# Loading ScalarE's joint table of logarithm and exponential by hand, in a fused two-model block

## What is computed

```python
def rms_norm(x, g):                      # norm1, norm2, pre/post norms, norms of q and k
    y = xf * lax.rsqrt(jnp.mean(xf * xf, axis=-1, keepdims=True) + EPS)
...
def forgetting_attention(q, k, v, fg_logit):     # 8 heads of 64, causal
    log_f = jax.nn.log_sigmoid(fg_logit)
    cum = jnp.transpose(jnp.cumsum(log_f, axis=1), (0, 2, 1))
    ...
        s = s + cum[:, :, start:end, None] - cum[:, :, None, :end]
        p = jax.nn.softmax(s, axis=-1)
...
def conformer_conv(...):                 # sigmoid gate, depthwise conv, layer_norm, silu
...
# the feed-forward part: silu(gate) * val
def retention(q, k, v):                  # 8 heads; ends in a group norm: rsqrt(var + EPS)
...
def diff_attention(q, k, v, lam):        # 8 heads, two softmaxes each
    p = jax.nn.softmax(jnp.where(mask, sc, neg), axis=-1)
    w = p[:, :, 0] - lam * p[:, :, 1]
...
o = rmsnorm(o, sub_norm_b[j]) * (1.0 - lambda_init)
y = (o * jax.nn.silu(gate)) @ w_out_b[j]
```

## Time and profile before

| | |
|---|---|
| median of 3 runs | 3242.74 us (3241.93 to 3243.2) |
| the profiled execution's own time | 3246.35 us |
| its span, first to last instruction | 3244.7 us |
| mean granted TensorE clock | 0.939 of 2.4 GHz |
| TensorE matmuls busy | 2837.1 us |
| VectorE busy | 1677.9 us |
| ScalarE busy | 745.0 us |

### The profile page before, as it was taken

One profiled execution on the slowest core, in us unless ns is written; L12 is line 12 of the kernel. 1 busy time (PEld: TensorE's weight loads), 2 busy tenths in 40 slices (PEclk: granted clock), 3 DMA queues, 4 the chain that ended last, 5 costly groups with the idle time before them and its releaser, 6 DMA issues.

```text
span 3244.7 us, 35199 instructions
## 1 busy us (share of the span) xinstructions
PE 2837.1 (87%) x13202; PEld 2246.1 (69%) x13202; DVE 1677.9 (52%) x2240; ACT 745.0 (23%) x1220; POOL 110.6 (3%) x124
## 2 busy tenths in 40 slices
PE   5518999797899999998999999999977999999785
PEld 4406666486787877876788888888865777777564
DVE  5671444425545555456444544544474666666534
ACT  3224434202111111112101110111042333333321
POOL 0330000000000000000000000000000000000000
PEclk9758999798999999999999999999988999999887
DMA  3101110032434344332322222222242222222121
GB/s 137 65 0 65 53 43 34 14 143 91 143 117 151 120 160 148 118 142 93 141 78 78 78 78 90 78 78 73 83 156 81 65 68 65 65 68 65 42 104 65
DMA packets 48617, 286.58 MB, mean 88 GB/s; under 512 B 6577, under 2 KB 6705, under 8 KB 18609
## 3 DMA queue, kind: packets, MB, share of 16 engines
q1 hardware_dynamic: 22064, 119.01, 10.8%
q0 software_dynamic: 14544, 105.91, 9.5%
q10 hardware_dynamic: 11952, 60.89, 4.9%
HBM read 248.03 MB, written 29.36 MB: 85 GB/s over the span
## 4 chain that ended last, share of the span: by engine, by line
PE 77%; DVE 14%; issue 4%; ACT 3%; DMA 1%; SPq 0%; DVEq 0%; ACTq 0%
PE PB L238 11%; PE PB L239 11%; PE PB L240 11%; PE OBB L238 8%; PE OBB L239 7%; PE OBB L240 7%; PE OBB L908 5%; PE PB L868 4%; PE TBB L822 4%; DVE cacc L727 2%; PE TBB L238 2%; PE TBB L239 2%; PE TBB L240 2%; DVE small L1069 1%; DVE V L1458 1%
## 5 line engine op out<-in xcount | busy, mean ns | idle before, releaser
L238 PE MATMUL PB<-HH,WH 128*128 128x512 f32 x1520 | 601.0, 395 | 40.9 <-DVE HL L370 16.1
L239 PE MATMUL PB<-HL,WH 128*128 128x512 f32 x1520 | 595.7, 392 | 0.0
L240 PE MATMUL PB<-HH,WL 128*128 128x512 f32 x1520 | 595.3, 392 | 0.0
L238 PE MATMUL OBB<-HH,WH 128*128 128x512 f32 x992 | 404.0, 407 | 6.1 <-DVE WL L254 6.1
L239 PE MATMUL OBB<-HL,WH 128*128 128x512 f32 x992 | 389.9, 393 | 0.0
L240 PE MATMUL OBB<-HH,WL 128*128 128x512 f32 x992 | 389.9, 393 | 0.0
L238 PEld LDWEIGHTS PB<-HH,WH 128*128 128x128 f32 x1520 | 288.2, 190 | 109.3 <-issue 41.0
L239 PEld LDWEIGHTS PB<-HL,WH 128*128 128x128 f32 x1520 | 288.2, 190 | 61.7 <-issue 2.0
L240 PEld LDWEIGHTS PB<-HH,WL 128*128 128x128 f32 x1520 | 287.9, 189 | 60.8
L254 DVE TENSOR_TENSOR WL<-RAW,WH 128x2048 fp32r<-128x2048 f32 x101 | 230.7, 2284 | 69.9 <-DMA WH<-units 53.7
L1012 ACT ACTIVATE E<-PB,small 128x128 f32<-128x128 f32 (+3 forms) x192 | 142.1, 741 | 430.4 <-DVE small L1072 430.4
(11 more groups left out here) (298 smaller groups left out, 3725.1 us busy)
## 6 DMA issues: line engine op xcount, KB each, us to landing
WH<-units POOLq DMA_DIRECT2D x85, 1024.0 KB, 5.0
RAW<-units SPq DMA_DIRECT2D x85, 1024.0 KB, 4.7
gs<-units ACTq DMA_DIRECT2D x16, 1024.0 KB, 4.7
gu<-gs ACTq DMA_DIRECT2D x16, 1024.0 KB, 3.9
RAW<-gu SPq DMA_DIRECT2D x16, 1024.0 KB, 4.8
WH<-gu POOLq DMA_DIRECT2D x16, 1024.0 KB, 5.1
tmpd<-xr SPq DMA_DIRECT2D x128, 64.0 KB, 2.0
A<-xT SPq DMA_DIRECT2D x4, 1024.0 KB, 12.4
```

Of the source, the lines that this page charges most:

```text
L238: first = pe.e.matmul(out, wh, xh, start=start, stop=False)
L239: pe.e.matmul(out, wh, xl, start=False, stop=False)
L240: return pe.e.matmul(out, wl, xh, start=False, stop=stop), first
```

## The change

```diff
+LN_EXP = "natural_log_exp_and_others"
...
 def root_act(act, squares):            # norm1, norm2
...
+            act.e.preload_act_table_set(LN_EXP)
             act.e.wait_ge(pe_done, at_mark(act, "pe", "total"))
             roots(act, PB[0], rbn)
...
 def norm_a_act(act, ph):
...
             spill(act)
+            act.e.preload_act_table_set(LN_EXP)
             act.e.wait_ge(pe_done, at_mark(act, "pe", "total"))
             roots(act, TBB, rbx)
...
 def total_act(act, ph, out):           # post_a, post_b
             act.start(ph)
+            act.e.preload_act_table_set(LN_EXP)
             act.e.wait_ge(pe_done, at_mark(act, "pe", "total"))
             roots(act, TBB, out)
...
 def mix_act(act, ph):
...
                 act.e.activation(sbm[:, c, :], cacc[:, c, :], ACT.Square).then_inc(act_done, act.mark(f"csq{c}"))
+            act.e.preload_act_table_set(LN_EXP)
             act.e.wait_ge(pe_done, at_mark(act, "pe", "var1"))
             act.e.wait_ge(dve_done, at_mark(act, "dve", "cum_lo"))
...
 def attend_act(...):
...
             if not forget:
                 e.wait_ge(dve_done, at_mark(act, "dve", "rawg1", i))
                 e.activation(sg[:, :], sg[:, :], ACT.Silu).then_inc(act_done, act.mark("silu"))
+                e.preload_act_table_set(LN_EXP)
             if more:
...
 def first_act(act, ph, forget):        # both attentions
             act.start(ph)
+            act.e.preload_act_table_set(LN_EXP)
             if not forget:
                 act.e.wait_ge(pe_done, at_mark(act, "pe", f"new{KT - 1}"))
                 roots(act, OBB, rbx)
```

## The result

| | before | after |
|---|---|---|
| median of the runs beside each other (5 each) | 3242.74 us (3241.12 to 3245.73) | 3225.01 us (3222.3 to 3226.84) |
| profiled execution, its own time | 3246.35 us | 3225.01 us |
| its span, mean granted clock | 3244.7 us, 0.939 | 3223.3 us, 0.942 |

The ratio is 0.9944 [0.9929, 0.9958]: 17.7 us faster (the interval reaches from 13.6 to 23.0 us), where 18.1 were forecast. Against the profiled execution of before the gain is 21.4 us of span, because that execution was 3.6 us above its median and this one is at its own.

What follows compares the result with a forecast made beforehand. TensorE, busy 87% of the span, was taken to bound the kernel, so only ScalarE loads on the chain count: 14 loads x 1.29 = 18.1 us, from 3242.74 to 3224.6 us. The range was 3213 to 3232.

Steps and rivals of the forecast that it cites:

- The sum, 14 loads by 1.29 us, 18.1 us: Whole kernel: of the loads removed, 14 were on the path at 1.29 us each, 18.1 us in all.
- norm2, post_a, post_b, two loads each: Norms over the model width: both loads leave the path, the new one hidden under TensorE's total; 6 loads together.
- last head, two: Last differential head: no projection left, TensorE waits 5.27 us for L1885, and both loads are in that wait.
- norm1, mix and the first attention, four loads, 5.16 us: Path loads saved: norm1's exponential load, mix's L640 load, and two behind the first attention's k0 and k1 logarithms.
- norm_a, nothing: Norm_a: no gain, as the chain goes through the 17.92 us spill of A and the root is done long before.
- Attention loop, 24 loads, nothing: Attention loop: its 24 loads gain nothing, as the exponentials end 3.4 us before TensorE wants them.
- heads, 14 loads, nothing: Differential heads in the loop: 14 loads gain nearly nothing, taken as 0, at most 0.3 us in two or three heads.
- First differential head, two loads: First differential head: both loads saved, new load within 16.5 us of ScalarE idle, everything behind serial, so all should travel.
- rival 1: Gain caught by a DMA or projection in first attention, first differential head or post_a: 6 loads lost, 3232.4 us; 12%.
- The copy of q, cost 0 by 9.8 us of cover: Differential heads: the new load delays q's copy (L1059) by 1.28 us, but its readers start 9.8 us later; cost 0.
- Rival 2, the clock: TensorE's clock shifts across the loop's seven heads: 3209.6 us if all at 1.00, 3230.6 if none; same mix expected; 16%.
- Rivals 3, 4 and 5: Joint table slower, 3260.6 us (2%); loads ignored, 3242.7 (3%); a switch holding ScalarE twice its row, 3206.6 (2%).

Runs made afterwards that it cites:

- the twenty switches: Changed kernel with twenty more loads in post_b behind the wait for TensorE's sum, alternating Exp and joint table: 3249.32 us, ratio 1.0015.
- the two opposite kernels: Changed kernel with separate Ln and Exp loads only in the loops, 3224.79 us (0.9949), or only on the path, 3241.53 us (0.9997).
- the kernel with the loops' tables apart: Changed kernel with separate Ln and Exp loads again in the attention loop and the loop of differential heads: 3224.79 us, ratio 0.9949.

## Why the prediction was right

- **The sum, 14 loads by 1.29 us, 18.1 us.** Measured 17.7, and 18.3 when these 14 were put back with three beside the path. The price was tested alone, by the twenty switches (1.288 us), and which loads count by the two opposite kernels. That the total came within 0.4 us is in part luck. The interval of the measurement, 13.6 to 23.0 us, would fit 11 to 17 loads; the places one by one are the better evidence. And between the two profiled executions the rows without a load moved by -1.47, +2.45, +0.56 and +0.76 us, which the sum put at nothing.
- **norm2, post_a, post_b, two loads each; last head, two.** Right: 2.65, 3.03, 2.67 and 2.56 us. The cover of the new load in post_b is larger than the 1.28 us needed, with 2.49 us to spare; and with that cover taken away the load behind the wait costs what the text said, about one load for each place.
- **norm1, mix and the first attention, four loads, 5.16 us.** 6.80 in the two executions. The loads are gone from the chain in each place. The rest, 1.6 us, is not theirs: from norm1 to the attention's first kT, TensorE's clock is at 1.2 GHz for 128.2 us before and 123.3 after, and executions of the changed kernel's code differ there by 1.1 us among themselves (248.57 to 249.66 us).
- **norm_a, nothing.** Right: the spill is on the chain at the same distance from its surroundings.
- **Attention loop, 24 loads, nothing; heads, 14 loads, nothing.** Right within the 1.6 us by which the kernel with the loops' tables apart differs. The 2.45 us that the heads' stretch took less is not theirs, but the clock's.
- **First differential head, two loads, "so all of it should travel".** This step failed by 1.2 us up to the transposes in the profiled execution, though the clock gave as much back just behind them. The text named rotation, swaps and VectorE as serial and took their length as fixed; the first swap grew from 1.98 to 3.26 us, because it came forward into the next weight load. It is rival 1 in small, at one of its three places, and for a reason that the row would have shown: the load's issue at 2455.88 stood 6.3 us ahead of the swap in the trace of before.
- **The copy of q, cost 0 by 9.8 us of cover.** Right in its result, wrong in its reason. The text named the Square as queued behind the copy, but priced only the copy. What decides is the chain from the Square to the scaling: 6.2 us of room on average, and 1.5 us of waiting per head once 7.7 us are added; the rest of the 2.5 is clock.
- **Rival 2, the clock.** Its expectation of the same mix held for the seven heads of the loop: two of the seven heads in the loop run their 16 matmuls in 2.05 us in both kernels (other heads 3.4 to 3.8), so two at the full 2.4 GHz before and two after. They are other heads, though: after they are these of the chain, before the ones that start this piece at 2632.90 and 2868.20.

```profile
2699.09 2.05 PE OBB L913 x16
...
2934.49 2.05 PE OBB L913 x16
```

  Outside these seven the clock did move: at the edges of the heads' stretch for some 2 us of gain, in the first attention for 1.5 us of loss. The forecast had neither; they happen to cancel in part.

- **Rivals 3, 4 and 5** fell: 741 ns as before, 60 loads in all with none at the lines named, and 0.01 us behind a load.

Open is what made the clock fall and rise where it did. The heads' stretch is 626.7 us in three kernels and 624.2 to 624.9 in the changed kernel and the one with the loops' tables apart, with 73 and 67 to 68 us at 1.2 GHz. In the three long ones at least one load of the first head's root stands behind TensorE's sum, in the others none; that this is the reason isn't shown. No run was made to move the clock alone.

## What to carry to other kernels

Count the loads of a table that stand on the chain, not those of the list: here a net 45 went and 14 carried the gain, and the two kernels that divide them show it (41 us of ScalarE for nothing that could be measured, 22 for 18 us). A load belongs in front of the wait for the operand, where it runs under the producer, and functions that follow each other directly belong in one table. When an engine off the bound gets faster, look at what DMA is in flight a microsecond or two ahead of the next transfer on its chain; and when an instruction is delayed, price each one queued behind it, down to the first whose reader is the bounding engine. Where two executions differ by a few microseconds in a stretch whose work is the same, compare the bounding engine's busy time and granted clock there before looking for a cause in the edit.

## What was not expected of the hardware

Three things. A 1 MB load of weights holds the DMA engines at a share of 0.97 in a window of its 6.1 us (0.88 in the next, together with the swap), and a swap of four times 64 KB in that time takes 2.6 to 3.4 us where it takes 1.98 alone. Where TensorE waited 10.6 us more in seven heads, its matmuls were busy 9.9 us longer as well, at a granted clock of 0.93 instead of 0.95. And switches in series have no seam: 20 of them took 25.77 us, 1.288 each, whichever of the two tables was loaded.
